# Four of 192 expert weight units loaded as 112 + 8 + 8 partitions instead of 128

## The chip, the cores and the metric

The kernel runs on one core of a Trainium2 chip. A core has TensorE (PE in the profile), VectorE (DVE), ScalarE (ACT), GpSimd (POOL) and SyncE (SP), and sixteen DMA engines that move data between device memory and the on-chip buffer of 128 partitions. The metric is the device time of the launch in microseconds; lower is better. All data are fp32.

## The reference

Two layers work on 256 latent tokens (and 256 context tokens in the first), each 1024 wide. Layer 0 mixes tokens by differential attention, layer 1 by multi-scale pooling. After each mixer comes the same mixture of experts:

```python
for i in range(2):
    yl = diff_attention(...) if i == 0 else pool_mixer(...)
    xl = deepnorm_update(xl, yl, g1, ...)
    tokens = xl * (1 + sc2) + sh2
    y2 = moe_ffn(tokens, router_w, router_b, moe_wg[i], moe_wu[i], moe_wd[i])
    xl = deepnorm_update(xl, y2, g2, ...)

def moe_ffn(h, ...):           # 16 experts, top 2 of one group of 4 for each token
    # for the tokens routed to expert e:
    (silu(xb @ wg[e]) * (xb @ wu[e])) @ wd[e]      # each weight is 1024 x 1024 fp32
```

Each layer reads 16 x 3 matrices of 4 MB. These 402 MB are most of what the launch reads.

## The kernel before

Each engine has its own program, written out in order, and they meet at semaphores. Every expert is computed for 64 token slots. Its three matrices come in six *units*: unit v holds half of a matrix (512 of its 1024 rows), 2048 KB, laid out so that partition p holds four consecutive rows, 16 KB that are contiguous in memory and on chip. So there are 96 units a layer, 192 in all, and one extra unit between the layers for the pooling weights.

The units go into a ring of eleven slots (`RING = 11`). SP issues the loads strictly in order of v (`load_unit`). Before it issues unit v it waits until TensorE has finished unit v - 11, whose slot it takes (`slot_free`, `used`). TensorE waits before each unit until it has landed: `landed` waits on the slot's semaphore. A load adds 16 to that semaphore when all of it has come, so the n-th unit in a slot is there at 16 n. The last expert's units 3 and 5 are loaded in two halves (`LAST_UNITS`); all others with one DMA instruction of 128 partitions.

On TensorE each expert is: units 0 to 3 (gate and up product, 64 matmuls), the gathering of tokens for the pair to come, the transposition of the hidden values, the scatter of the expert before, and units 4 and 5 (down product, 32 matmuls). VectorE and ScalarE apply the activation and gates between these. Between layer 0 and layer 1 the pooling mixer runs, a stretch in which TensorE takes no expert unit.

Early in layer 0, in attention, ACT issues 16 small DMAs that copy 32 partitions of 4 KB each from one quarter of the partitions to another (`swapped`), beside the loads from SP. They appear below as `ring<-ring ACTq`.

Of the kernel before, what the change touches and what calls it, by code (L numbers as in the profile page):

```python
# [26 lines left out]
P = 128  # L27
# [20 lines left out]
RING = 11  # L48
FREE = (10, 4, 8, 5, 9, 6, 7, 1, 0, 2, 3)
UNIT = 4096  # L50
EU = 6
# [24 lines left out]
LAYER_BASE = [0, POOL_UNIT + 1]  # L76
PAIRS = NE // 2
LAST_UNITS = tuple(LAYER_BASE[1] + (NE - 1) * EU + n for n in (3, 5))


GROUPS = [(kind, j, t) for j in range(2) for kind, n in (("k", 4), ("q", 2), ("v", 4)) for t in range(n)]

# [142 lines left out]
def trunk(nc, x, tokens, cond, hbias, bias_rows, scale_rows, mod_w, attn_wqkv, attn_wo, attn_lam, attn_subln,  # L225
          pool_w, router_w, router_b, moe_wg, moe_wu, moe_wd, consts, rope, band, out):
    with ExitStack() as st:
# [5 lines left out]
        def sem(name):  # L233
            if name not in sems:
                sems[name] = st.enter_context(nc.semaphore(name))
            return sems[name]
# [50 lines left out]
        def slot(s):  # L287
            return ring[:, s * UNIT:(s + 1) * UNIT]
# [65 lines left out]
        def ring_slot(v):  # L354

            return FREE[v % RING], v // RING + 1

        def landed(eng, v):

            s, n = ring_slot(v)  # L360
            eng.wait_ge(sem(f"ring_loaded_{s}"), 16 * n)

        def used(eng, v):

# [46 lines left out]
        def first_unit(layer, e):  # L411

            return LAYER_BASE[layer] + e * EU
# [32 lines left out]
        def _(sp):  # L446
            def load(dst, src, s):
                sp.dma_start(dst, src).then_inc(s, 16)
# [50 lines left out]
            def slot_free(v):  # L499

                if v < AHEAD:
                    return
                if v == 1:
                    early_used(sp, ("v", 1))
                elif v == 2:
                    sp.wait_ge(sem("row_done"), 4)
                elif v in (3, 4):
                    sp.wait_ge(sem("scores_done"), NS)
                elif v == 5:
                    sp.wait_ge(sem("pv_done"), NS)  # L510
                elif v == 6:
                    sp.wait_ge(sem("oT_done"), 2 * TT)
                elif v in (7, 8):
                    early_used(sp, ("wo", v - 7))
                elif v == 9:
                    sp.wait_ge(sem("half_summed"), 2 * (NSUM - 1))
                elif v == LATE_UNIT:
                    sp.wait_ge(sem("job_done"), EARLY_JOBS + 1)
                else:
                    used(sp, v - RING)  # L520

            def load_unit(layer, e, n):

                v = first_unit(layer, e) + n
                slot_free(v)
                s, _ = ring_slot(v)
                src = (moe_wg, moe_wu, moe_wd)[n // 2][layer, e, (n % 2) * HALF:(n % 2 + 1) * HALF, :]
                to, of = slot(s).rearrange("p (k n) -> p k n", k=4), src.rearrange("(p k) n -> p k n", p=P)
                if v in LAST_UNITS:
                    load(to[:, 0:2], of[:, 0:2], sem(f"last_first_{n}"))  # L530
                    load(to[:, 2:4], of[:, 2:4], sem(f"ring_loaded_{s}"))
                else:
                    load(to, of, sem(f"ring_loaded_{s}"))

            def load_expert(layer, e):
                for n in range(EU):
                    v = first_unit(layer, e) + n
                    if v >= ISSUED and v != LATE_UNIT:
                        load_unit(layer, e, n)
                    if v == AFTER_UNIT:  # L540
                        load_unit(0, LATE_UNIT // EU, LATE_UNIT % EU)

            for what in LOADS:
                if what == "rows":
                    load_rows()
                elif what == "ahead":
                    for n in range(AHEAD):
                        load_unit(0, 0, n)
                elif what == "x":
                    load(xn[:, :].rearrange("p (t n) -> p t n", t=TT), x[0].rearrange("(t p) n -> p t n", p=P), sem("x_loaded"))  # L550
                elif isinstance(what, tuple) and what[0] == "e":
                    load_unit(0, what[1] // EU, what[1] % EU)
                elif isinstance(what, tuple):
                    load_early(what)
                else:
                    load_sum_unit(what)
# [12 lines left out]
            for layer in range(DEPTH):  # L569
# [3 lines left out]
                if layer == 0:  # L573
                    slot_free(POOL_UNIT)
                    s, _ = ring_slot(POOL_UNIT)
# [29 lines left out]
        def _(pe):  # L605
# [388 lines left out]
            def ring_unit(v):  # L994
                landed(pe, v)
                return slot(ring_slot(v)[0]).rearrange("p (k n) -> p k n", k=4)

            def last_unit(b, lhs, v, n, k0):

                w = slot(ring_slot(v)[0]).rearrange("p (k n) -> p k n", k=4)  # L1000
                pe.wait_ge(sem(f"last_first_{n}"), 16)
                two_halves(b, lhs, w, k0, range(2))
                landed(pe, v)
                return two_halves(b, lhs, w, k0, range(2, 4))
# [79 lines left out]
            def pool_layer():  # L1084

                v = POOL_UNIT
                pe.wait_ge(sem("pool_loaded"), 16)
                landed(pe, v)
                w = slot(ring_slot(v)[0])
                pw = w[:, 0:2048].rearrange("p (k n) -> p k n", k=KT)  # L1090
# [779 lines left out]
```

## Time and profile before

| | us |
|---|---|
| median of 3 runs | 1183.56 |
| lowest, highest | 1182.87, 1183.60 |
| the profiled execution, whole | 1182.86 |
| its span, first to last instruction | 1181.2 |
| TensorE busy in the span | 1123.7 |
| VectorE busy | 364.3 |
| ScalarE busy | 167.1 |

The profiled execution lasts 1.7 us more than its span. It has 480.17 MB moved by DMA, 476.18 MB of it read from memory. A DMA moves in *packets*, each handled by one DMA engine; for an expert unit a packet is the 16 KB of one partition. The "DMA share" of a stretch is the time that all packets took there, divided by sixteen engines times the stretch; it can pass 1 slightly, since packets of one engine overlap a little. Busy time of TensorE is modelled, so that a high share alone doesn't say that it sets the pace.

### The profile page before, as it was taken

What the parts mean: (1) busy time and instruction counts of PE and PEld (TensorE: products, weight loads), DVE (VectorE), ACT (ScalarE), POOL (GpSimd) and SP (SyncE); (2) the same over time, 40 slices, a digit from 0 to 9 for tenths busy, and PEclk for the clock granted to TensorE, in tenths of its full rate; (3) what the DMA queues carried; (4) which work ended last, traced back from release to release, by engine and by line L of the source; (5) the groups of instructions that cost most, each with busy time, mean ns of one, the idle gap of its engine ahead of it and who ended that gap; (6) DMA issues with size and microseconds to landing.
All of it is one profiled execution on the core that took longest, in us unless ns stands there. A gap on an engine that the chain in (4) does not pass through costs nothing.

```text
span 1181.2 us, 12432 instructions
## 1 busy us (share of the span) xinstructions
PE 1123.7 (95%) x5290; PEld 487.3 (41%) x5290; DVE 364.3 (31%) x737; ACT 167.1 (14%) x396; POOL 8.0 (1%) x10
## 2 busy tenths in 40 slices
PE   8999999989999999999988889999999999988885
PEld 3554645553443343333333237443334333333321
DVE  1579999773111111111111125111111111111113
ACT  1201337240000010000000005100001000000000
POOL 0000000000000000000000010000000000000000
PEclk9999999999999999999999999999999999999998
DMA  9999999959999999999999999999999999999994
GB/s 383 402 365 413 361 316 369 390 225 398 428 431 429 432 430 431 430 431 429 431 429 432 432 423 430 409 431 431 430 430 431 432 429 431 428 432 431 431 428 187
DMA packets 41449, 480.17 MB, mean 407 GB/s; under 512 B 5168, under 2 KB 6448, under 8 KB 9776
## 3 DMA queue, kind: packets, MB, share of 16 engines
q1 hardware_dynamic: 40336, 476.91, 96.2%
q10 hardware_dynamic: 1056, 2.43, 0.7%
q8 instruction: 44, 0.72, 0.2%
q14 instruction: 13, 0.11, 0.0%
HBM read 476.18 MB, written 1.05 MB: 404 GB/s over the span
## 4 chain that ended last, share of the span: by engine, by line
PE 63%; DMA 24%; DVE 10%; issue 1%; ACT 0%; another core or an unknown queue 0%; SPq 0%; DVEq 0%; ACTq 0%
PE ps L959 42%; DMA ring<-in_moe_wu 19%; DMA ring<-in_mod_w 5%; PE ps L951 5%; PE ps L967 4%; DVE ring L1406 3%; PE ps L803 2%; DVE extra L1406 1%; PE ps L977 1%; DVE modp L1406 1%; DVE small L1538 1%; PE ps L639 1%; PE ps L703 1%; PE ps L901 1%; PE ps L983 1%
## 5 line engine op out<-in xcount | busy, mean ns | idle before, releaser
L959 PE MATMUL ps<-ring,tra 128*64 128x512 f32 x2048 | 454.3, 598 | 25.5 <-DMA ring<-in_moe_wu 19.6
L959 PEld LDWEIGHTS ps<-ring,tra 128*64 128x64 f32 x2048 | 146.5, 138 | 325.2 <-issue 283.0
L959 PE MATMUL ps<-ring,work 128*64 128x512 f32 x1024 | 226.8, 595 | 1.9 <-DVE work L1776 1.9
L959 PEld LDWEIGHTS ps<-ring,work 128*64 128x64 f32 x1024 | 71.6, 137 | 135.6 <-issue 133.3
L1298 ACT ACTIVATE work<-ps 128x512 f32<-128x512 f32 x32 | 19.1, 598 | 511.4 <-PE ps L959 511.4
L1769 DVE TENSOR_TENSOR work<-ps,work 128x512 f32<-128x512 f32 x32 | 22.1, 692 | 204.7 <-ACT work L1298 204.7
L1774 DVE TENSOR_TENSOR work<-work,ps 128x512 f32<-128x512 f32 x32 | 22.0, 688 | 201.8 <-PE ps L959 201.8
L1291 ACT ACTIVATE tra<-ps,cols 128x128 f32<-128x128 f32 x128 | 48.2, 457 | 254.7 <-PE ps L951 254.7
L951 PEld LDWEIGHTS ps<-extra,xn 128*128 128x128 f32 x512 | 61.0, 195 | 24.3 <-issue 22.7
L951 PE MATMUL ps<-extra,xn 128*128 128x128 f32 x512 | 66.9, 285 | 1.4 <-DVE extra L1675 1.4
L967 PE MATMUL ps<-work,extra 64*128 64x512 f32 x256 | 63.6, 615 | 1.6 <-DVE work L1782 1.6
L703 PE MATMUL ps<-ring 128*128 128x512 f32 x128 | 58.6, 601 | 0.7 <-ACT ring L1164 0.6
L1406 DVE SCALAR_TENSOR_TENSOR ring<-ring,cols 128x512 f32<-128x512 f32 x63 | 47.4, 752 | 2.2
L1782 DVE TENSOR_TENSOR work<-ps,rows 128x512 f32<-128x512 f32 x16 | 11.1, 692 | 107.9 <-PE ps L959 107.9
L1782 DVE TENSOR_TENSOR work<-ps,gt 128x512 f32<-128x512 f32 x16 | 11.1, 692 | 104.9 <-PE ps L959 104.9
L1776 DVE COPY work<-ps 128x512 f32<-128x512 f32 x32 | 22.1, 692 | 51.0 <-PE ps L977 51.0
L703 PEld LDWEIGHTS ps<-ring 128*128 128x128 f32 x128 | 23.1, 190 | 31.5 <-issue 31.5
L1406 DVE SCALAR_TENSOR_TENSOR modp<-ring,cols,modp 128x512 f32<-128x512 f32 x42 | 31.6, 752 | 1.5
L967 PEld LDWEIGHTS ps<-work,extra 64*128 64x128 f32 x256 | 22.0, 186 | 22.1 <-issue 15.1
L1757 DVE COPY extra<-ps 128x256 f32<-128x256 f32 x32 | 13.6, 424 | 47.3 <-PE ps L983 47.3
L706 PE MATMUL ps<-ring 128*128 128x512 f32 x64 | 28.1, 592 | 0.0
L709 PE MATMUL ps<-ring 128*128 128x256 f32 x128 | 28.1, 379 | 0.0
(196 smaller groups left out, 715.7 us busy)
## 6 DMA issues: line engine op xcount, KB each, us to landing
ring<-in_moe_wg SPq DMA_DIRECT2D x64, 2048.0 KB, 29.8
ring<-in_moe_wu SPq DMA_DIRECT2D x63, 2048.0 KB, 28.9
ring<-in_moe_wd SPq DMA_DIRECT2D x63, 2048.0 KB, 30.1
ring<-in_mod_w SPq DMA_DIRECT2D x42, 1024.0 KB, 11.0
ring<-in_attn_wqkv SPq DMA_DIRECT2D x4, 2048.0 KB, 15.4
ring<-in_mod_w SPq DMA_DIRECT2D x3, 2048.0 KB, 18.7
ring<-in_attn_wo SPq DMA_DIRECT2D x2, 2048.0 KB, 12.2
ring<-ring ACTq DMA_DIRECT2D x16, 128.0 KB, 8.1
```

The costliest lines, as they stand in the source:

```text
L703: return mm(bank(acc_bank(g)), w[:, k, t * P:t * P + P], hT[:, k, :], start=first, stop=end)
L706: return mm(bank(acc_bank(g)), hT[:, k, t * P:t * P + P], rhs, start=first, stop=end)
L709: last = mm(bank(acc_bank(g), 0, P, n * TOK, (n + 1) * TOK), w[:, k, hd * P:hd * P + P], hT[:, k, 0:TOK], start=first and n == 0, stop=end ...
L803: last = mm(bank(2 * t + h), oT[t][:, k, :], wo[:, k, :], start=(k == 0), stop=(k == KT - 1))
L951: last = mm(bank(bk, 0, P, k * P, k * P + slots), xn[:, c0:c0 + P], sgat[:, t, 0:slots], start=(t == 0), stop=(t == TT - 1), skip_group_ch ...
L959: last = mm(ps[SLOTS * h:SLOTS * h + SLOTS, b, :], lhs(k0 + k), w[:, k, h * NB:(h + 1) * NB], start=(k0 + k == 0), stop=(k0 + k == KT - 1) ...
L967: last = mm(bank(2 * t + h), sw[SLOTS * h:SLOTS * h + SLOTS, t * P:t * P + P], ysb[SLOTS * h:SLOTS * h + SLOTS, :], start=False, stop=True ...
L1291: nc.scalar.activation(xg[i // 2 % 2][:, kk, :], bank(bk, k * P, k * P + P), ACT.Identity, bias=one(bcol[2 * layer], kk, 1), scale=one(aco ...
L1406: ins = v_.scalar_tensor_tensor(out=acc, in0=w[:, k, :], scalar=ck, in1=acc, op0=ALU.mult, op1=ALU.add)
L1769: v_.tensor_tensor(hmid, bank(4), sig, ALU.mult).then_inc(sem("silu_ready"), 1)
L1776: v_.tensor_copy(work[:, NB:2 * NB], bank(7)).then_inc(sem("hTt_copied"), 1)
L1782: v_.tensor_tensor(ysb, bank(6), gt[layer], ALU.mult).then_inc(sem("ys_ready"), 1)
```

## The change

`UNEVEN` names four units, always the first unit (n = 0, a half of the gate matrix) of an expert: experts 6 and 10 of layer 0, experts 2 and 8 of layer 1. Such a unit is loaded with three DMA instructions: partitions 0 to 111, then 112 to 119, then 120 to 127, all on the same semaphore. `landed` counts 48 instead of 16 for each such unit. The bytes are the same.

```diff
+UNEVEN = tuple(LAYER_BASE[0] + e * EU for e in (6, 10)) + tuple(LAYER_BASE[1] + e * EU for e in (2, 8))
+EVEN_ROWS, REST_ROWS = 112, 8
...
         def landed(eng, v):
             s, n = ring_slot(v)
-            eng.wait_ge(sem(f"ring_loaded_{s}"), 16 * n)
+            more = sum(2 for u in UNEVEN if u <= v and u % RING == v % RING)
+            eng.wait_ge(sem(f"ring_loaded_{s}"), 16 * (n + more))
...
-                if v in LAST_UNITS:
+                if v in UNEVEN:
+                    load(to[0:EVEN_ROWS], of[0:EVEN_ROWS], sem(f"ring_loaded_{s}"))
+                    for p0 in range(EVEN_ROWS, P, REST_ROWS):
+                        load(to[p0:p0 + REST_ROWS], of[p0:p0 + REST_ROWS], sem(f"ring_loaded_{s}"))
+                elif v in LAST_UNITS:
```

SP's program before, at experts 5 to 7 of layer 0 (each row is a run of DMA instructions, tile<-tensor, partitions x elements, and what the first waits for):

```order
L448 DMA ring<-in_moe_wg 128x4096 [waits unit_used] x2
L448 DMA ring<-in_moe_wu 128x4096 [waits unit_used] x2
L448 DMA ring<-in_moe_wd 128x4096 [waits unit_used] x2
L448 DMA ring<-in_moe_wg 128x4096 [waits unit_used] x2
L448 DMA ring<-in_moe_wu 128x4096 [waits unit_used] x2
```

And with the change, at the same place:

```order
L452 DMA ring<-in_moe_wu 128x4096 [waits unit_used] x2
L452 DMA ring<-in_moe_wd 128x4096 [waits unit_used] x2
L452 DMA ring<-in_moe_wg 112x4096 [waits unit_used]
L452 DMA ring<-in_moe_wg 8x4096 x2
L452 DMA ring<-in_moe_wg 128x4096 [waits unit_used]
L452 DMA ring<-in_moe_wu 128x4096 [waits unit_used] x2
```

One instruction has become three, the two new ones without a wait of their own and ahead of the expert's other five units. The same stands at the three other places. The programs of the other engines keep every instruction and its order; only the numbers that TensorE waits for have changed.

## Rows read from the trace of the kernel before

**Rows 1.** The page: span, DMA rate in 40 slices, queues
```profile
span 1181.2 us, 12432 instructions
GB/s 383 402 365 413 361 316 369 390 225 398 428 431 429 432 430 431 430 431 429 431 429 432 432 423 430 409 431 431 430 430 431 432 429 431 428 432 431 431 428 187
q8 instruction: 44, 0.72, 0.2%
```
**Rows 2.** The chain that ended last: start us, us, what
```profile
524.15 39.25 DMA ring<-in_moe_wu
...
575.47 46.32 DMA ring<-in_moe_wu
...
997.16 40.36 DMA ring<-in_moe_wu
...
1049.59 46.55 DMA ring<-in_moe_wu
```
**Rows 3.** Waits of PE from 262 to 524 us: total us, times, longest
```profile
PE ps L959 <- DVE work L1776: 0.9, 1, 0.9
```
**Rows 4.** Waits of PE from 524 to 690 us
```profile
PE ps L959 <- DMA ring<-in_moe_wu: 10.0, 8, 1.7
PE ps L959 <- DMA ring<-in_moe_wg: 3.0, 4, 1.1
```
**Rows 5.** Windows: us, busy us (x instructions) by engine, PEclk, DMA share, GB/s
```profile
310.00:500.00 190.00, 190.00 (x942) 75.81 (x940) 33.04 (x83) 14.72 (x35) 0.00 (x0) 0.99 1.01 430
524.00:684.00 160.00, 145.88 (x696) 53.34 (x692) 21.17 (x45) 11.10 (x24) 0.00 (x0) 1.00 1.01 431
...
769.00:965.00 196.00, 196.00 (x958) 76.99 (x955) 32.65 (x71) 15.33 (x36) 0.00 (x0) 1.00 1.01 431
```
**Rows 6.** DMA view, 769 to 965 us
```profile
DMA packets 5792, 84.41 MB, mean 431 GB/s; under 512 B 640, under 2 KB 640, under 8 KB 640
q8 instruction: 8, 0.13, 0.2%
```
**Rows 7.** Windows at the end of the last load, same columns
```profile
1158.00:1161.00 3.00, 2.60 (x14) 1.28 (x14) 0.95 (x2) 0.00 (x0) 0.00 (x0) 1.00 0.89 377
1161.00:1162.00 1.00, 1.00 (x8) 0.43 (x8) 0.00 (x0) 0.00 (x0) 0.00 (x0) 1.00 0.54 229
1162.00:1163.00 1.00, 1.00 (x8) 0.31 (x6) 0.00 (x0) 0.00 (x0) 0.00 (x0) 1.00 0.48 205
1163.00:1164.00 1.00, 1.00 (x6) 0.29 (x4) 0.00 (x0) 0.00 (x0) 0.00 (x0) 1.00 0.29 123
1164.00:1165.00 1.00, 1.00 (x8) 0.40 (x6) 0.00 (x0) 0.00 (x0) 0.00 (x0) 1.00 0.04 16
```
**Rows 8.** DMA view, 740 to 760 us: share in tenths, 0.5 us each
```profile
DMA  9979999656669598999999999999999999999998
```
**Rows 9.** DMA view, 57 to 63 us, and the page's issue row of these copies
```profile
DMA packets 438, 1.76 MB, mean 293 GB/s; under 512 B 116, under 2 KB 167, under 8 KB 282
q1 hardware_dynamic: 289, 1.38, 77.6%
q10 hardware_dynamic: 149, 0.39, 23.9%
...
ring<-ring ACTq DMA_DIRECT2D x16, 128.0 KB, 8.1
```
**Rows 10.** DMA view, 70 to 75.5 us
```profile
DMA packets 325, 1.63 MB, mean 296 GB/s; under 512 B 76, under 2 KB 76, under 8 KB 177
```
**Rows 11.** SP's DMA instructions on ring, 560 to 640 us: ns min/median/max
```profile
L448 SPq DMA_DIRECT2D ring<-in_moe_wg x6: 328/3961/4240, 560.0 to 621.3; - x6
```
**Rows 12.** DMA view, 310 to 500 us: issues, KB, median us to landing
```profile
ring<-in_moe_wg SPq DMA_DIRECT2D x14, 2048.0 KB, 25.7
```

## The prediction

> **What bounds the kernel now.** I read the page first, then the chain of waits, the waits of TensorE by stretch, and the windows of the DMA. TensorE is busy for 1123.7 of 1181.2 us, which looks like a compute bound; the chain and the DMA rate say otherwise. From slice 11 of 40 on, the DMA moves 428 to 432 GB/s in nearly every slice [rows 1], and the DMA share is 1.01 in the long windows [rows 5]: the sixteen engines never rest. In 262 to 524 us TensorE doesn't wait for a load at all [rows 3]; it lives on the units that had landed ahead, and a unit takes 25.7 us from issue to landing, five units' worth of queue [rows 12]. From 524 us on the lead is used up. TensorE waits for loads 12 times, 13.0 us in all [rows 4], and the chain steps from one load to the next, 39.25 and 46.32 us each [rows 2]. Layer 1 repeats it: no lead left from 997 us on, loads of 40.36 and 46.55 us in the chain [rows 2]. So both layers end at the pace of the DMA, and as the DMA was busy without a pause before, a microsecond that it loses anywhere in a layer, even where TensorE isn't waiting, is missing at that layer's end. Which engine is meant matters: TensorE may start a unit only when all sixteen engines have delivered their share, so the end follows the slowest DMA engine, not the mean.
>
> Price of a packet: 84.41 MB in 5792 packets, 640 of them tiny, is 5152 packets of 16.4 KB [rows 6]. One engine moves 430 / 16 = 26.9 GB/s [rows 5], so a packet takes 0.61 us, and an even unit (8 packets on each engine) 4.88 us.
>
> Are the sixteen engines level? No. The last load ends at 1165 us, but from 1161 us on the share is 0.54, 0.48, 0.29 and 0.04 in one microsecond each [rows 7]: about half of the engines have finished by 1161, the other half works on. The sum, 1.35 us x 16 = 21.6 engine-microseconds over eight engines, is a mean lag of 2.7 us, and the last is near 4. The same is to be seen between the layers: for some 2.5 us from 743.5 us on, the share is 0.6 instead of 1 [rows 8], since one half has emptied its queue and the other hasn't. I take 3 us of lead for the faster half, at the end of each layer. What makes it is the instruction fetches, as I read it: 44 packets [rows 1], 8 of them in 196 us [rows 6], which come on top of the loads; spread over all engines they would make no halves, so they seem to fall on eight engines only. No view here numbers the engines.
>
> **The change part by part.**
>
> Issues. SP gets eight more DMA instructions. An issue takes 0.33 us where the queue has room and 3.96 where it is full [rows 11]; then it waits for the queue and not the queue for it. With loads issued 25.7 us ahead [rows 12] this is hidden. Its price if the cover were gone is 8 x 0.33 = 2.6 us. I count nothing. TensorE's waits are as many as before.
>
> Packets. In a changed unit the 112 partitions give seven packets to each engine, the two parts of 8 give one each to eight engines, if both parts take the same eight. Those carry 9, the others 7, against 8: 0.61 us more on eight engines and 0.61 less on the rest, twice a layer, 1.22 us. If the nine fall on the faster half, the slow half gets 1.22 us earlier in each layer and the fast one stays ahead by 3 - 2.44 = 0.56 us: 2 x 1.22 = 2.4 us gained. If they fall on the slow half, 2.4 us lost.
>
> The Trainium skill (DMA: Bandwidth & Descriptors, Why a DMA increments its semaphore by 16 and not by 1) says that an SP transfer is split over the largest number of engines up to 16 that divides its partitions, the lowest-numbered ones: 16 for 112, the same eight for both parts of 8. No run here shows it yet.
>
> Narrow transfers. This is what decides. All eight packets of a part go into eight neighbouring partitions. Does it matter how few partitions are written at once? The trace has one kind of narrow transfer, the 32-partition copies on q10. While they run, all queues together move 1.76 MB in 6 us, 293 GB/s [rows 9], and in another such stretch 296 [rows 10], though the engines count as busy (77.6 + 23.9%). At 430 GB/s it would be 2.58 MB: 0.82 MB or 1.9 us are lost in 6 us, in which q10 moved 0.39 MB, three copies of 128 KB. That is 0.64 us lost for each, beside the 0.30 us that its bytes need: it costs 3.1 times its bytes. The packets of the loads from SP are drawn out with it, so the copies aren't just slow themselves; something that both share is crowded. The copies read and write on chip, which the 8-partition parts do not, and that may be part of it.
>
> For the 8-partition parts, also 128 KB each, I bound the stretching of a packet from below by 1 (no crowding) and from above by 8 (the eight packets one after another, 4.9 us for a part). Nearest row: 3.1 at 32 partitions, with two partitions to an engine. Eight partitions are narrower, so I take 4. Then each of the two packets takes 2.44 us instead of 0.61, 3.66 us more, and with the extra packet 0.61 the eight engines lose 4.27 us in each changed unit, 8.5 us in a layer. If these are the engines that lead by 3 us, 5.5 us of it remain at the layer's end; 11.1 us in both. Layer 0's loss moves the start of layer 1 as a whole (pooling stands between), so the two add up.
>
> The Trainium skill (SBUF — State Buffer, Door 1: The DMA port swizzle) gives the reason: sixteen ports of some 27 GB/s take the DMA's writes, four neighbouring partitions share one, and transfers into 0 to 3 were measured at 27.6 GB/s. By this rule a part of 8 uses two ports and lasts 131072 B / 54.4 GB/s = 2.4 us, an estimate from the page that lands on the same sum. The 293 GB/s beside the copies go along with it, without proving it.
>
> Sum. 1182.86 for the profiled execution + 11.1 = 1194.0; the median of the runs is 0.7 us higher, so 1194 to 1195. I forecast 1194: slower by 0.9%.
>
> **The rivals.**
>
> Balance, on the other side. A packet into narrow partitions costs 0.61 us like any other, and the nines fall on the half that leads. Then 2.4 us come off if the fast half keeps a lead in both layers, about 1.9 if its slowest engine were only 1.9 us ahead in one layer (there 1.9 - 1.22 = 0.7 us would be the gain). Median 1183.56 - 2.4 = 1181.1 to 1181.7. For it: the halves in rows 7 and 8 are just as large (3 us) as what two changed units move (2.44), and a memory load, not an on-chip copy, may not be crowded by what crowds the copies. Against it: rows 9 and 10. It turns into the forecast's opposite when a narrow packet is stretched less than about 1.5 times: then the eight leaders lose 1.22 + 4 x 0.31 = 2.4 us a layer, within their 3.
>
> Wrong half. No crowding, but the nines fall on the engines that are behind: 1183.56 + 2.4 = 1186.0. Nothing in the views tells the halves apart.
>
> Crowding on the engines behind. As the forecast but without the lead to use up: 4 x 4.27 = 17.1 us, 1200.7. The same time comes with a stretching of 5 and a lead: 5.5 us in a unit, 11 in a layer, 8 after the lead, 16 in all.
>
> The 112 partitions crowd too. Seven partitions to an engine may no longer be spread as eight are. If each of these packets were stretched by a half, 2.1 us more in each unit, 8.5 in all: 1202 to 1203 on top of the forecast.
>
> **How the numbers follow.** Crowding in one of its forms 0.52 (forecast 0.27 with 1189 to 1198 as its own range, the two worse rivals 0.25), balance 0.34, wrong half 0.10, nothing to be measured 0.04. Comparisons of this kernel tell a change from none at about 0.2%, 2.4 us. The balance rival sits on this line: I give 0.13 to more than 2.4 us gained and 0.21 to less. Wrong half divides likewise. Faster 0.13, same 0.30, slower 0.57. The range must reach to the balance rival, which holds a third of the chance, and up over the worse crowding: 1181 to 1203.
>
> **What would show it.** Forecast right: in windows of 5 us in which the changed units are fetched, the GB/s fall below 430 for some microseconds with the share still near 1; TensorE's waits after 524 us grow by about 5 us in each layer. At the end of the load (rows 7) the halves are changed over, with the eight that were first now last. Balance right: GB/s stays at 430 through the changed units, the shares of rows 7 fall from 1 to 0 within 2 us instead of 4, the dip of rows 8 is shallower, and the waits of rows 4 shrink by about a microsecond. Wrong half: shares as in rows 7, but drawn out over 6 us. The forecast is wrong if the narrow parts don't lower the rate. If SP's issues counted, SP would issue later than TensorE frees the slots in 262 to 524 us, with a queue shorter than 25.7 us.

## The result, and the profile after

The changed kernel takes 1220.9 us (median of four runs, 1216.2 to 1224.5) against 1183.4: slower by 3.1%, ratio 1.031 (95% interval 1.0294 to 1.0325). The forecast was 1194, its range ended at 1203. The sign was right and the size three times too small: 37.5 us instead of 11. One run of e3 below (1674 us, at a granted clock of 0.65) is left out of its time.

The page of the changed kernel, the same rows as in [rows 1] where they exist, and the kinds of issue:

```profile
span 1220.7 us, 12440 instructions
GB/s 385 389 395 411 345 299 402 362 224 430 431 432 420 335 430 430 432 294 431 431 428 431 429 425 421 293 430 431 431 431 431 299 431 432 428 430 431 432 430 136
q8 instruction: 44, 0.72, 0.2%
...
ring<-in_moe_wg SPq DMA_DIRECT2D x60, 2048.0 KB, 38.4
...
ring<-in_moe_wg SPq DMA_DIRECT2D x4, 1792.0 KB
```

From slice 10 on the rate is 420 to 432 GB/s, but for four slices of 30.5 us (and the last), where it falls to 335, 294, 293 and 299. Each of the four holds one of the changed units. Windows of 50 us around them (us, busy us by engine, PEclk, DMA share, GB/s):

```profile
380.00:430.00 50.00, 50.00 (x260) 19.54 (x258) 8.45 (x20) 3.78 (x10) 0.00 (x0) 1.00 1.01 368
505.00:555.00 50.00, 36.02 (x162) 12.71 (x160) 5.04 (x12) 2.71 (x6) 0.00 (x0) 0.90 1.01 347
750.00:800.00 50.00, 48.34 (x259) 25.68 (x258) 11.95 (x46) 9.42 (x22) 0.00 (x0) 0.97 0.96 340
940.00:990.00 50.00, 42.66 (x194) 15.52 (x192) 6.25 (x15) 2.71 (x6) 0.00 (x0) 0.90 1.01 350
```

Against 430 and 431 in the long windows of before [rows 5], what is missing in bytes is 50 x (1 - 368/430) = 7.2 us of DMA time, then 9.7, 10.5 and 9.3. In three of the windows the share is 1.01: the engines count as busy, each packet only takes longer.

The third window (share 0.96) also holds the dip between the layers. It is in the kernel before too [rows 8], there outside 750 to 800. First the dips (before, after) and what is left of the third window, then the last 21 us of all loads (before, after):

```profile
743.00:751.00 8.00, 8.00 (x40) 2.65 (x38) 0.69 (x1) 0.79 (x2) 0.00 (x0) 1.00 0.89 352
761.00:769.00 8.00, 8.00 (x40) 2.75 (x38) 1.60 (x6) 1.81 (x5) 0.00 (x0) 1.00 0.69 262
769.00:800.00 31.00, 30.05 (x153) 13.35 (x150) 4.35 (x9) 2.11 (x5) 0.00 (x0) 1.00 1.01 330
...
1144.00:1165.00 21.00, 17.98 (x84) 5.98 (x82) 2.07 (x3) 2.08 (x3) 0.00 (x0) 1.00 0.86 366
1183.00:1204.00 21.00, 17.82 (x82) 5.86 (x80) 2.07 (x3) 2.08 (x3) 0.00 (x0) 1.00 0.70 296
```

The third unit itself costs 31 x (1 - 330/430) = 7.2 us. The dip costs 3.1 us instead of 1.5, the last 21 us cost 6.5 instead of 3.1. So the four units lose 7.2 + 9.7 + 7.2 + 9.3 = 33.4 us and the two layer ends (the dip and the last 21 us) 5.1 us more than before: 38.5 us. The profiled execution's span is 39.5 us longer than that of before (1220.7 against 1181.2).

The first of the four from near, in windows of 2 us:

```profile
392.00:394.00 2.00, 2.00 (x12) 0.63 (x10) 0.00 (x0) 0.00 (x0) 0.00 (x0) 1.00 0.97 418
394.00:396.00 2.00, 2.00 (x11) 0.62 (x8) 0.12 (x1) 0.00 (x0) 0.00 (x0) 1.00 1.15 369
396.00:398.00 2.00, 2.00 (x8) 0.54 (x9) 1.65 (x4) 0.00 (x0) 0.00 (x0) 1.00 1.01 238
398.00:400.00 2.00, 2.00 (x12) 0.70 (x10) 0.12 (x1) 0.00 (x0) 0.00 (x0) 1.00 1.05 246
400.00:402.00 2.00, 2.00 (x12) 0.59 (x10) 0.00 (x0) 0.00 (x0) 0.00 (x0) 1.00 1.08 229
402.00:404.00 2.00, 2.00 (x12) 0.72 (x10) 0.00 (x0) 0.05 (x1) 0.00 (x0) 1.00 1.25 164
404.00:406.00 2.00, 2.00 (x12) 0.69 (x10) 0.69 (x1) 0.55 (x1) 0.00 (x0) 1.00 0.88 123
406.00:408.00 2.00, 2.00 (x12) 0.60 (x10) 0.00 (x0) 0.00 (x0) 0.00 (x0) 1.00 0.81 172
408.00:410.00 2.00, 2.00 (x12) 0.72 (x10) 0.00 (x0) 0.00 (x0) 0.00 (x0) 1.00 0.89 319
410.00:412.00 2.00, 2.00 (x15) 1.30 (x12) 0.69 (x1) 0.00 (x0) 0.00 (x0) 1.00 0.99 426
```

The mean time of a packet is 16 engines x share x 16.4 KB / rate. Before 394 it is 0.61 us. Through the 112-partition part (about 394 to 402, by the order of the loads; no view names the partitions) it is 16 x 1.01 x 16.4 / 238 = 1.1 us, then about where the parts of 8 come it is 2.0 and 1.9 us, as a mean over all engines. In lost time: (1720 - 1082) / 430 x 2 = 3.0 us in the first four windows of the episode, (1720 - 778) / 430 x 2 = 4.4 us in the four after it.

TensorE waits for nothing while this happens at 394 to 410: it is busy for the whole of every window. It pays later. Its waits from 524 to 710 us (total, times, longest), which answer to [rows 4]:

```profile
PE ps L967 <- DMA ring<-in_moe_wu: 13.1, 11, 1.2
PE ps L967 <- DMA ring<-in_moe_wg: 11.9, 6, 8.2
PE ps L967 <- DMA ring<-in_moe_wd: 2.3, 1, 2.3
```

27.3 us instead of 13.0, one of them 8.2 us long, at the second changed unit (531 to 540 us). The end of the last load, to be held against [rows 7]:

```profile
1195.00:1198.00 3.00, 2.16 (x12) 0.50 (x8) 0.69 (x1) 0.00 (x0) 0.00 (x0) 1.00 0.71 300
1198.00:1199.00 1.00, 0.89 (x6) 0.80 (x8) 0.13 (x1) 0.00 (x0) 0.00 (x0) 1.00 0.19 82
...
1201.00:1202.00 1.00, 1.00 (x6) 0.29 (x4) 0.00 (x0) 0.00 (x0) 0.00 (x0) 1.00 0.06 25
1202.00:1203.00 1.00, 1.00 (x8) 0.41 (x6) 0.00 (x0) 0.00 (x0) 0.00 (x0) 1.00 0.06 25
```

The two halves of before are gone. A share of 0.06 is one engine of sixteen (1/16 = 0.0625), and one works alone for the last microseconds.

### The profile page after: what moved, and what is told of

The parts are those of the page before. It is cut to its first block, busy times and chain, and to the rows that moved or that the text cites. A ratio compares the mean times of both kernels' runs of the same rounds, so it can differ in the third digit from the quotient of the medians.

```text
span 1220.7 us, 12440 instructions
## 1 busy us (share of the span) xinstructions
PE 1130.6 (93%) x5290; PEld 487.0 (40%) x5290; DVE 364.1 (30%) x737; ACT 167.4 (14%) x396; POOL 8.0 (1%) x10
## 4 chain that ended last, share of the span: by engine, by line
PE 54%; DMA 31%; DVE 12%; issue 1%; another core or an unknown queue 1%; ACT 0%; SPq 0%; DVEq 0%; ACTq 0%
PE ps L967 35%; DMA ring<-in_moe_wu 23%; PE ps L959 4%; DMA ring<-in_moe_wd 4%; PE ps L975 4%; DVE ring L1414 3%; DMA ring<-in_mod_w 3%; PE ps L811 2%; DVE modp L1414 2%; DVE extra L1414 1%; DVE small L1546 1%; PE ps L985 1%; PE ps L711 1%; PE ps L909 1%
## 5 line engine op out<-in xcount | busy, mean ns | idle before, releaser
L967 PE MATMUL ps<-ring,tra 128*64 128x512 f32 x2048 | 461.3, 602 | 55.6 <-DMA ring<-in_moe_wu 31.8
```

The lines of the kernel that those rows point to most:

```text
L967: last = mm(ps[SLOTS * h:SLOTS * h + SLOTS, b, :], lhs(k0 + k), w[:, k, h * NB:(h + 1) * NB], start=(k0 + k == 0), stop=(k0 + k == KT - 1) ...
```

## The experiments

All but the last have the base of the changed kernel and differ in how the named units are split; each unit stays 2048 KB. A list entry is (first partition, end, step, first column, end column) of one DMA. Times are medians; a ratio compares with runs of the kernel before on the same chip in the same session. Differences are ratio minus one, times 1184.

**e1, 112 + 16**

```diff
-    112 + 8 + 8
+    PARTS = [(0, 112, 1, 0, UNIT), (112, P, 1, 0, UNIT)]
```

> The same four units, but the last 16 partitions come in one DMA: 112 + 16, eight packets on each of the sixteen engines. Crowding theory (transfers to part of the partitions run at a fraction of the rate because several engines write to the same group of partitions): the 112 part costs what it costs in the changed kernel, the 16 part has sixteen engines on 16 partitions and costs about half of what two parts of 8 cost, so roughly 7 us a unit, 28 us in all, 1211. Imbalance theory (nine packets against seven): no imbalance is left, 1183.5.

Measured 1214.2, ratio 1.0252 (1.0235 to 1.0270). By the dealing that the prediction assumes no engine has more packets than another here, and four fifths of the loss are still there. The imbalance isn't its main cause.

**e2, 64 + 64**

```diff
+    PARTS = [(0, 64, 1, 0, UNIT), (64, P, 1, 0, UNIT)]
```

> The four units as 64 + 64 partitions, again eight packets on each engine. Crowding by partition groups: sixteen engines share half of the groups, each packet takes twice 0.61 us, a unit 9.8 instead of 4.9 us, plus 4.9 us x 4 = 20 us, 1203. If only the parts of 8 are dear: 1183.5. Imbalance theory: 1183.5.

Measured 1213.8, ratio 1.0234 (1.0209 to 1.0260), 28 us, more than the 20 expected. Two large, even halves, and nearly the same price. Windows of 5 us at the first unit:

```profile
390.00:395.00 5.00, 5.00 (x26) 2.05 (x27) 1.12 (x2) 1.51 (x4) 0.00 (x0) 1.00 1.00 429
395.00:400.00 5.00, 5.00 (x25) 1.61 (x22) 0.19 (x1) 0.00 (x0) 0.00 (x0) 1.00 1.08 308
400.00:405.00 5.00, 5.00 (x22) 1.49 (x22) 1.70 (x4) 0.00 (x0) 0.00 (x0) 1.00 0.99 213
405.00:410.00 5.00, 5.00 (x26) 1.72 (x24) 0.69 (x1) 0.60 (x1) 0.00 (x0) 1.00 0.98 220
```

213 and 220 GB/s are half of 430: all sixteen engines at work, each packet at twice its time. The window from 380 to 430 us has 375 GB/s, which is 6.4 us lost where 4.9 were expected: the half rate lasts longer than the unit's own bytes need.

**e3, three DMAs of all partitions**

```diff
+    PARTS = [(0, P, 1, 0, 3584), (0, P, 1, 3584, 3840), (0, P, 1, 3840, UNIT)]
```

> Control: the four units in three DMAs as well, but each over all 128 partitions (14 KB, 1 KB and 1 KB of every row), with the same semaphore counts. Crowding theory: no change, within 1 us (1183.5). If the number of DMA instructions or the shared semaphore of three transfers is what costs: near 1221.

Measured 1184.2, ratio 1.0004 (0.9993 to 1.0016). Three instructions and the counts on the semaphore cost nothing.

**e4, only one unit changed**

```diff
-UNEVEN = tuple(LAYER_BASE[0] + e * EU for e in (6, 10)) + tuple(LAYER_BASE[1] + e * EU for e in (2, 8))
+UNEVEN = (LAYER_BASE[0] + 6 * EU,)
```

> 112 + 8 + 8 in one unit only, the first of expert 6 in layer 0. It lies where TensorE has a lead of several units. If the loss is a fixed loss of DMA time for each such unit, and DMA time is what ends the layer: a quarter of the change's 37.5 us, 9.4 us, 1193. If the loss comes from TensorE waiting at the changed unit itself, the lead hides it and this one is free: 1183.5.

Measured 1191.2, ratio 1.0066 (1.0045 to 1.0087): 7.8 us, for a unit at which TensorE does not wait. Its window has

```profile
380.00:430.00 50.00, 50.00 (x262) 19.54 (x260) 8.45 (x20) 3.61 (x9) 0.00 (x0) 1.00 1.01 372
```

which is 6.7 us of lost DMA time. TensorE's waits for loads between 380 and 700 us are 20.5 us, against 13.0 in 524 to 690 before [rows 4], where it had none until 524 [rows 3]. A loss in the stretch where TensorE has a lead is paid at the layer's end, in full as far as the interval (5.3 to 10.3 us) tells.

**e8, even and odd partitions**

```diff
+    PARTS = [(0, P, 2, 0, UNIT), (1, P, 2, 0, UNIT)]
```

> The four units as two DMAs of 64 partitions, the even ones and the odd ones. Together a DMA reaches all sixteen groups of partitions, where 64 neighbours (e2) reach half of them. If only the number of groups that a DMA reaches counts: no loss, 1184. If what counts is how many engines are at one group at the same time, and a DMA deals its partitions out in runs of four consecutive rows to each engine, the engines still meet two by two: about as e2, 1212.

Measured 1183.5, ratio 0.9997 (0.9988 to 1.0007). The DMAs are as large as those of e2 and have as many packets to an engine; only the step is 2. The same windows as for e2:

```profile
395.00:400.00 5.00, 5.00 (x22) 1.50 (x20) 1.90 (x4) 0.00 (x0) 0.00 (x0) 1.00 1.02 433
400.00:405.00 5.00, 5.00 (x26) 1.68 (x24) 0.54 (x1) 0.60 (x1) 0.00 (x0) 1.00 1.01 429
405.00:410.00 5.00, 5.00 (x26) 1.62 (x24) 0.15 (x1) 0.00 (x0) 0.00 (x0) 1.00 1.01 433
```

So where the rows lie decides, not how many there are. (Partition p takes its 16 KB from the p-th 16 KB of the unit in every run, so the rows of e8 lie apart in memory as well as on chip; e10 bears on which side counts.) My own idea of how a DMA deals partitions to the engines (runs of neighbours) would have given e2's loss here and is wrong for this shape.

**e9, 96 + 32**

```diff
+    PARTS = [(0, 96, 1, 0, UNIT), (96, P, 1, 0, UNIT)]
```

> The four units as 96 + 32 partitions, six and two packets on each engine. Crowding: near 112 + 16 and 64 + 64, about 7 us a unit, 1208 to 1214. If the cost came from the narrowness of the smaller part alone, 32 partitions would cost half of what 16 cost, 1198.

Measured 1215.6, ratio 1.0275 (1.0255 to 1.0294), 33 us. Three ways to cut at a partition (112 + 16, 96 + 32, 64 + 64) cost 30, 33 and 28 us: hardly a matter of where the cut is.

**e5 and e6, small pieces spread and close**

```diff
 e5 PARTS = [(0, P, 1, 0, 3584)] + [(b + r, b + r + 29, 4, 3584, UNIT) for b in range(0, P, 32) for r in range(4)]
 e6 PARTS = [(0, P, 1, 0, 3584)] + [(b, b + 8, 1, 3584, UNIT) for b in range(0, P, 8)]
```

> The four units as one DMA of all 128 partitions for the first 14 KB of each row, and sixteen DMAs of eight partitions for the last 2 KB, where the eight partitions of one DMA lie four apart (0, 4, ..., 28; 1, 5, ..., 29; and so on to 99, 103, ..., 127). Eight engines carry 0.7 us more than in an even unit, eight 0.6 us less, about as in the changed kernel. Crowding by groups of four neighbouring partitions (the Trainium skill, SBUF - State Buffer, Door 1): each of the eight packets goes to a group of its own, so almost nothing is lost: 1183 to 1187. If any transfer to few partitions is slow, wherever they lie, it costs what the close ones cost (e6). Balance theory, if the busier eight are those that lead: 1181.5.

> The same seventeen DMAs for each of the four units, same sizes and engines, but the eight partitions of one DMA are neighbours (0 to 7, 8 to 15, ...). Crowding by groups of four: four engines write to one group; 2 KB packets take four times 0.08 us, sixteen of them 3.6 us more in a unit, plus the 0.7: 4.3 us x 4 = 17 us, less up to 6 us for the lead of the eight engines: 1194 to 1201. If where the partitions lie doesn't matter: the same as e5.

Measured 1194.5, ratio 1.0094 (1.0079 to 1.0109), and 1197.7, ratio 1.0127 (1.0090 to 1.0164). The order is the expected one, but the intervals overlap and e5 is dearer than its expectation. At the first unit the two do differ as expected: 422 GB/s in e5 from 380 to 440 us, 1.1 us lost, and 405 in e6, 3.5 us lost. What makes e5 dear is in part issue. After pooling, where the queue is short, SP needs these times for 18 DMAs (start, us; e5, then e6), and e5's engines run dry (last row):

```profile
751.69 11.59 SPq L452 DMA_DIRECT2D ring<-in_moe_wg  x18
758.23 6.22 SPq L452 DMA_DIRECT2D ring<-in_moe_wg  x18
...
760.00:765.00 5.00, 4.05 (x25) 2.21 (x25) 1.02 (x2) 1.50 (x4) 0.00 (x0) 1.00 0.43 112
```

A DMA with its eight partitions four apart took SP 0.62 us in the median, one of eight neighbours 0.30. So this pair compares more than the place of the rows; e10 and e11 repeat it with whole rows.

**e10 and e11, whole rows spread and close**

```diff
 e10 PARTS = [(b + r, b + r + 29, 4, 0, UNIT) for b in range(0, P, 32) for r in range(4)]
 e11 PARTS = [(b, b + 8, 1, 0, UNIT) for b in range(0, P, 8)]
```

> The four units in sixteen DMAs of eight whole rows (16 KB packets), the eight rows four apart. Eight engines then carry all sixteen packets of each, 9.8 instead of 4.9 us. If each of the eight packets has a group of partitions of its own, the loss is this imbalance, less what the engines' lead covers, plus some meeting with the other half in partitions 64 to 127: 4 x 5 to 4 x 7 us, 1200 to 1212. If narrowness by itself is slow: as e11.

> The same sixteen DMAs for each of the four units, but eight neighbouring rows in each. With the 2.2 us that a packet of the 8-row parts takes in the changed kernel, eight engines need 16 x 2.2 = 35 us for a unit, 30 more than before: four times that, 120 us, about 1300. If it makes no difference how the rows lie: as e10.

Measured 1234.1, ratio 1.0391 (1.0351 to 1.0432), and 1263.0, ratio 1.0639 (1.0602 to 1.0677). Close rows cost 29 us more than spread ones with the same count of instructions and packets, although SP issues the spread ones more slowly (0.62 against 0.30 us). The absolute prices were off on both sides: 120 expected for e11 and 76 found, 16 to 28 expected for e10 and 46 found. Part of both prices is not a lower rate but idle engines. At the end of layer 0 the share falls to one half (e10, then e11), as it would if the eight engines with all the packets were still at work and the others had finished, and in e10 it is 0.63 from 780 to 790 us, while SP issues the small DMAs.

```profile
705.00:710.00 5.00, 3.80 (x18) 1.06 (x16) 0.00 (x0) 0.59 (x2) 0.00 (x0) 1.00 0.50 211
715.00:720.00 5.00, 3.80 (x20) 1.19 (x18) 0.00 (x0) 0.37 (x2) 0.00 (x0) 1.00 0.50 215
```

The two episodes, e10 first, in windows of 4 us:

```profile
396.00:400.00 4.00, 4.00 (x19) 1.30 (x16) 0.23 (x1) 0.00 (x0) 0.00 (x0) 1.00 1.02 434
400.00:404.00 4.00, 4.00 (x18) 1.20 (x18) 1.66 (x4) 0.00 (x0) 0.00 (x0) 1.00 1.08 426
404.00:408.00 4.00, 4.00 (x20) 1.29 (x18) 0.00 (x0) 0.16 (x1) 0.00 (x0) 1.00 1.03 213
408.00:412.00 4.00, 4.00 (x22) 1.38 (x20) 0.69 (x1) 0.44 (x1) 0.00 (x0) 1.00 1.01 209
412.00:416.00 4.00, 4.00 (x26) 2.05 (x23) 0.69 (x1) 0.00 (x0) 0.00 (x0) 1.00 0.93 205
```

```profile
396.00:400.00 4.00, 4.00 (x18) 1.19 (x16) 1.31 (x3) 0.00 (x0) 0.00 (x0) 1.00 1.04 209
400.00:404.00 4.00, 4.00 (x20) 1.29 (x18) 0.58 (x3) 0.00 (x0) 0.00 (x0) 1.00 1.01 225
404.00:408.00 4.00, 4.00 (x22) 1.38 (x20) 0.69 (x1) 0.60 (x1) 0.00 (x0) 1.00 1.06 180
408.00:412.00 4.00, 4.00 (x22) 1.35 (x20) 0.00 (x0) 0.00 (x0) 0.00 (x0) 1.00 1.06 156
412.00:416.00 4.00, 4.00 (x28) 2.78 (x26) 0.97 (x2) 0.75 (x3) 0.00 (x0) 1.00 1.00 147
```

In e11 the rate halves at once at 396 us. In e10 it stays full for 8 us more, then halves for 12. That is what engines would do of which eight write partitions 0 to 63 on ground of their own, and then, in 64 to 127, meet the eight that already work there on later units. I read the order of the pieces into the windows; no view names the partitions. If it is right, it also speaks for the chip as the side where they meet: in memory the rows of 0 to 63 are spaced just as those of 64 to 127. No run moves a row in memory without moving it on chip, so this rests on e10 and on the on-chip copies of [rows 9].

**e12, the change with its last 16 partitions dealt by turns**

```diff
+    PARTS = [(0, 112, 1, 0, UNIT), (112, 127, 2, 0, UNIT), (113, P, 2, 0, UNIT)]
```

> The change with one thing different: the last sixteen partitions are dealt to the two small DMAs by turns (112, 114, ..., 126 and 113, 115, ..., 127), so that two engines instead of four meet at a group of four partitions. Packets, engines and counts are those of the change. Crowding by groups: the two packets take 1.2 us each instead of 2.2, 2.0 us less in a unit, 8 us in all, 1213. If the 112 part alone makes the loss: as the change, 1221.

Measured 1221.8, ratio 1.0292 (1.0255 to 1.0329; runs from 1212 to 1227). A miss: of the 8 us that I expected to get back about 2 are there, though intervals so wide leave room for most of them. The trace agrees with little: in 395 to 410 us of the first unit e12 has 236, 203 and 282 GB/s, 6.6 us lost, against 7.4 in the changed kernel (249, 174, 229), 0.8 less where 2.0 were expected. The expectation had put a packet of the small parts at 2.2 us, above the 1.9 to 2.0 of the windows. What exactly the two small parts owe to each other's neighbourhood stays open.

**e13 to e15, the imbalance without neighbours**

```diff
 e13 PARTS = [(1, P, 2, 0, UNIT), (2, P, 4, 0, UNIT)] + [(b, b + 29, 4, 0, UNIT) for b in range(0, P, 32)]
 e13 UNEVEN = (LAYER_BASE[0] + 10 * EU, LAYER_BASE[1] + 8 * EU)
 e14 PARTS = [(1, P, 2, 0, UNIT), (2, P, 4, 0, UNIT), (0, P, 4, 0, UNIT)]
 e15 PARTS = [(1, P, 2, 0, UNIT), (2, P, 4, 0, UNIT), (0, 29, 4, 0, UNIT), (32, 61, 4, 0, UNIT), (64, P, 4, 0, UNIT)]
```

> The imbalance of the change without its neighbours: one unit in each layer comes as the 64 odd partitions, 32 partitions four apart, and four times eight partitions four apart. Ten packets on eight engines and six on eight, which is what two changed units of a layer shift together. Balance theory, if the nines fell on the engines that lead: 2.4 us faster, 1181.4; if on the engines behind: 2.4 us slower, 1186. If the partitions' side takes no more than one engine's rate, moving a packet to another engine gives nothing, since the group of partitions that it goes to stays as busy: 1184 to 1186.

> Control: the four units in three DMAs of 64, 32 and 32 partitions with steps of 2, 4 and 4, eight packets on every engine, each DMA reaching all groups of partitions evenly. Crowding by groups: nothing lost, 1183.5 to 1184.5, as for the even and odd halves (e8). If every transfer of 32 partitions or fewer is slow by itself: 1195 or more.

> The four units with nine packets on eight engines and seven on eight, as in the change, but with steps: the 64 odd partitions, 32 four apart, two times 8 four apart in partitions 0 to 60, and 16 four apart in 64 to 124. Only this last part (one packet each) makes two engines meet at a group, 0.6 us. Crowding theory: 0 to 2 us a unit, 1184 to 1192, against 9.4 us a unit in the change. Balance theory with the nines on the leading half: 1181.5; with the nines behind: 1186. If nine against seven itself had made the loss: near 1221.

Measured: e13 (ten and six, one unit in each layer) 1191.0, ratio 1.0056 (1.0040 to 1.0072); e14 (eight and eight) 1185.2, ratio 1.0008 (0.9999 to 1.0017); e15 (nine and seven in four units) 1189.9, ratio 1.0048 (1.0033 to 1.0063). The control costs 1 us at most: steps of 4 and DMAs of 32 partitions are free. e15 has the very packet counts that the change was named for, and costs 5.7 us, 1.4 a unit, where the change costs 9.4. Its second window has 421 GB/s against the change's 347:

```profile
505.00:555.00 50.00, 49.99 (x248) 19.57 (x246) 8.05 (x18) 4.21 (x10) 0.00 (x0) 1.00 1.01 421
```

And neither e13 nor e15 gains anything from the shift. Their loads end worse, not better. The last 12 us up to the end of the last load, e14 and then e15:

```profile
1153.90:1165.90 12.00, 11.05 (x52) 3.88 (x50) 1.38 (x2) 0.00 (x0) 0.00 (x0) 1.00 0.72 304
1159.60:1171.60 12.00, 11.05 (x52) 3.88 (x50) 1.38 (x2) 0.00 (x0) 0.00 (x0) 1.00 0.43 181
```

That is 3.5 us of lost DMA time against 6.9. The same 12 us cost 3.0 in the kernel before, 3.3 in e3, 4.2 in e8 and 6.5 in e13 (one execution each).

**e16, the order of the copies in attention** (base: the kernel before)

```diff
-                    for n in range(4):
+                    for n in (0, 2, 1, 3):
```

> The kernel before, with the four 32-partition copies of each group of heads issued in the order 0, 2, 1, 3 instead of 0, 1, 2, 3, so that two that follow each other write to different halves of the partitions. Crowding by groups: engines that have gone on to the next copy no longer meet those of the one before; 16 copies that lose 0.64 us each leave at most 10 us to win, and most of it isn't on the path that sets the end: 1181 to 1184. If the crowding comes from within one copy alone: no difference, 1183.5.

Measured 1183.8, ratio 0.9995 (0.9984 to 1.0006). Its DMA rates in the stretches of [rows 9] and [rows 10]:

```profile
57.00:63.00 6.00, 6.00 (x30) 5.28 (x29) 1.07 (x2) 0.59 (x1) 0.00 (x0) 1.00 1.02 315
70.00:75.50 5.50, 5.50 (x15) 2.39 (x14) 3.92 (x6) 0.59 (x1) 0.00 (x0) 1.00 1.04 317
```

315 and 317 GB/s instead of 293 and 296: a little less crowding, in one execution each, and no time gained. No kernel here beats the one before.

## Why the prediction was right or wrong, point by point

**What bounds the kernel: right.** DMA time is what ends both layers. The lost DMA time (38.5 us by bytes) is nearly all of the 39.5 us by which the profiled execution is longer, and e4 shows it for a unit at which nothing waits.

**Issues and count: right.** e3 gives 0 for three instructions instead of one. With sixteen or seventeen it is another matter (e5, e10).

**The mechanism: right, and larger than the copies of attention showed.** e2 against e8 isolates the place of the rows: same DMA size, same packets, 28 us against none. That several engines meet at the same part of the buffer is the reading that fits this and e10; no view shows it. For the packets of the small parts I had taken four times 0.61 = 2.44 us; the windows give 1.9 to 2.0 as a mean over all engines.

**The 112 partitions: the first step that failed.** They stood in the sum at 0.61 us a packet; crowding of this part was only a rival, priced at half a packet more. It was 1.1 us, 3.0 us lost in the first unit, 12 in four if the others are like it. I looked at the narrowness of the small parts, but what counts is that a part isn't the whole of 128 partitions nor spread over them: 64 + 64 has no narrow part and costs 28 us.

**The lead: the second step that failed.** I charged the loss to eight engines and took off 3 us of lead in each layer, 6 us in all. There is no such credit. Lost bytes, counted over all sixteen engines, are paid as lost time (e4: 6.7 us of DMA time, 7.8 us of run time), and the ends of the layers, where the lead should have been used up, got 5.1 us longer; at the very end one engine is behind all the rest. Which engines hold the others up no view shows.

With these two the sum is 4 x (3.0 + 4.4) = 29.6 us. The rest is of two kinds. The second changed unit of each layer lost 9.7 and 9.3 us instead of 7.2, and the ends of the layers lost 5.1 us more than before. Why the second units are dearer was not tested. For the ends, nine packets against seven is a candidate, since e15 and e13 lengthen the last one as well (6.9 and 6.5 us), but so does e1 without that imbalance (239 GB/s in its last 12 us, 5.3 us lost).

**The rivals.** Balance: refuted. e15 and e13 have the imbalance almost alone and cost 5.7 and 6.6 us; at best the shift was worth something smaller than what their last bit of crowding took. e14 excludes that the steps did it. Their last loads lose 3 us more than those of the control e14, which speaks against the extra packets having fallen on the engines that lead, but no experiment got rid of the meeting in partitions 64 to 127, so it isn't settled. Wrong half: it fits these drawn-out ends, but was not tested by itself, and its 2.4 us are small beside 37. The rivals of crowding on the engines behind (1200.7) and of the crowding 112 (8.5 more) would have to be taken both, 1209, and still fall short by 12.

**The odds.** A third of the chance lay on the balance rival although [rows 9] already spoke against it, and the range ended at 1203 because each form of crowding was priced alone.

## What to carry to other kernels

A load that fills all 128 partitions, or a stepped set that runs over all of them, kept sixteen DMA engines at full rate here; one that covers a range of neighbours did not, not even half of the buffer. To split a load in a kernel that lives on DMA rate, cut along the columns (e3) or by steps of partitions (e8, e14), not at a partition. And in a kernel whose DMA never rests, price a slow transfer by the rate that all engines lose, wherever in the layer it stands, before counting who gets how many packets.

## What the runs showed of the hardware

- 128 partitions as 0 to 63 and 64 to 127 ran at 213 to 220 GB/s, as evens and odds at 429 to 433. The Trainium skill (SBUF — State Buffer, Door 1: The DMA port swizzle) says that partitions 0 to 63 reach eight of sixteen ports and no more than 0 to 31 do; the halved rate agrees. That an even-odd split costs nothing fits the rule only if each engine also stays at its own port, which no view shows.
- The prediction's estimate from the same page, two ports for a part of 8, means 2.4 us a packet; 1.9 to 2.0 was measured as a mean over all engines, some of which were elsewhere.
- The disturbance is wider than the unit: at the first changed unit the rate was back at 426 only from 410 us on, 16 us after its fall. In these 16 us 3.7 MB were moved, of which the unit is 2.1 MB, so loads of other units were slowed with it.
- Sixteen small DMAs in a row can leave the DMA engines idle where the queue is short: a share of 0.43 for 5 us after pooling in e5, 0.63 for 10 us in e10. In both a DMA of eight partitions four apart took SP 0.62 us in the median, one of eight neighbours 0.30 (e6, e11).
